# Attention scores of a latent-attention step: the fifth product of four heads as four 64-row matmuls in a row, with four score banks and two banks for turned probabilities

## The reference, cut to what matters

```
def mla_attend(q_abs, q_r, q_pos, ckv, kr, k_pos):
    s = (jnp.einsum('bqhr,bkr->bhqk', q_abs, ckv).astype(jnp.float32)
         + jnp.einsum('bqhp,bkp->bhqk', q_r, kr).astype(jnp.float32)) * SOFTMAX_SCALE
    mask = q_pos[:, None] >= k_pos[None, :]
    s = jnp.where(mask[None, None], s, NEG_INF)
    p = jax.nn.softmax(s, axis=-1).astype(ckv.dtype)
    return jnp.einsum('bhqk,bkr->bqhr', p, ckv)
```

## Time and profile before

| | us |
|---|---|
| median of 3 runs (2332.59 to 2333.3) | 2333.02 |
| the profiled execution | 2344.84 |
| its span | 2343.0 |
| PE busy (94% of the span) | 2205.3 |
| DVE busy (56%) | 1308.4 |
| ACT busy (43%) | 1002.9 |
| score matmuls (L842), 1600 of them, busy | 359.8 |
| value matmuls (L861), 816, busy | 211.5 |
| transposes (L852), 1088, busy | 137.6 |

### The profile page before, as it was taken

How to read it: one execution, slowest core, us unless ns; L and a number is a source line. 1 busy time by engine, 2 the same in 40 slices (tenths; PEclk the granted TensorE clock), 3 DMA queues, 4 the chain that set the end, 5 groups by cost and what they waited for, 6 DMA issues and landing times.

```text
span 2343.0 us, 33629 instructions
## 1 busy us (share of the span) xinstructions
PE 2205.3 (94%) x12021; PEld 2036.9 (87%) x12021; DVE 1308.4 (56%) x2647; ACT 1002.9 (43%) x1802; POOL 364.7 (16%) x500
## 2 busy tenths in 40 slices
PE   5999599999999998786999999999999999999997
PEld 4888478888888887665999999999999999999997
DVE  4565477788777776332644455444644464446445
ACT  3555456555555544322433343334333443344333
POOL 1333221111000010101400050004100420023001
PEclk9999799999999999887999999999999999999999
DMA  5454432111110010404453434443453345344533
GB/s 171 150 162 145 118 81 55 41 35 34 28 28 28 19 64 5 166 1 156 129 176 119 142 118 157 145 137 119 135 166 121 128 136 174 106 150 134 175 117 131
DMA packets 134866, 257.99 MB, mean 110 GB/s; under 512 B 18682, under 2 KB 84482, under 8 KB 133430
## 3 DMA queue, kind: packets, MB, share of 16 engines
q1 hardware_dynamic: 111454, 223.29, 29.3%
q10 hardware_dynamic: 20960, 20.19, 2.9%
q0 software_dynamic: 2304, 12.58, 1.4%
HBM read 213.45 MB, written 42.79 MB: 109 GB/s over the span
## 4 chain that ended last, share of the span: by engine, by line
PE 51%; DVE 1%; issue 1%; DMA 0%; ACT 0%; POOL 0%; DVEq 0%; POOLq 0%; SPq 0%; ACTq 0%
PE d_ps L112 50%; PE d_ps L1567 1%; DMA d_hf<-out_ht 0%; DVE d_gate_p L1518 0%; DVE d_mrg L80 0%; POOL d_fstat L1389 0%; DVE d_y L1481 0%; ACT d_mrg L1347 0%; ACT d_zs L1375 0%; DVE d_ya L1522 0%; DVE d_ht L80 0%; ACT d_ht L1293 0%; DVE d_pool L80 0%; DVE d_y L1556 0%; DVE d_y L1483 0%
## 5 line engine op out<-in xcount | busy, mean ns | idle before, releaser
L112 PE MATMUL d_ps<-d_ht,d_wr 128*128 128x412 f32 x3840 | 737.4, 350 | 22.2 <-DVE d_ht L80 22.1
L112 PEld LDWEIGHTS d_ps<-d_ht,d_wr 128*128 128x128 f32 x3840 | 718.3, 188 | 26.2 <-issue 22.6
L80 DVE TENSOR_TENSOR d_wr<-d_ws,d_wr 128x1024 fp32r<-128x1024 f32 x262 | 322.9, 1232 | 553.4 <-ACT d_wr L1288 553.3
L1288 ACT ACTIVATE d_wr<-d_ws 128x1024 fp32r<-128x1024 f32 x262 | 277.5, 1059 | 608.2 <-PE d_ps L112 598.9
L842 PE MATMUL b_ps<-kt,b_qs 128*128 128x512 f32 (+3 forms) x1600 | 359.8, 377 | 18.6 <-POOL b_qs L80 13.8
L842 PEld LDWEIGHTS b_ps<-kt,b_qs 128*128 128x128 f32 x1600 | 278.3, 195 | 65.2 <-POOL b_qs L80 14.3
L861 PE MATMUL b_ps<-b_pt,kv 128*128 128x512 f32 x816 | 211.5, 402 | 8.7 <-DVE b_pt L80 8.7
L80 DVE TENSOR_TENSOR b_pt<-b_ps,b_pt 128x512 fp32r<-128x512 f32 x272 | 171.9, 683 | 83.0 <-ACT b_pt L746 82.6
L739 ACT ACTIVATE b_p<-b_p,b_bias 128x1024 f32<-128x1024 f32 (+7 forms) x192 | 172.0, 898 | 103.8 <-DVE b_low L797 100.4
L746 ACT ACTIVATE b_pt<-b_ps 128x512 fp32r<-128x512 f32 x272 | 143.8, 596 | 146.6 <-PE b_ps L852 146.3
L861 PEld LDWEIGHTS b_ps<-b_pt,kv 128*128 128x128 f32 x816 | 153.6, 191 | 48.3 <-DVE b_pt L80 14.1
(11 more groups left out here) (193 smaller groups left out, 2289.4 us busy)
## 6 DMA issues: line engine op xcount, KB each, us to landing
d_ws<-in_w SPq DMA_DIRECT2D x264, 512.0 KB, 3.5
out_q<-a_qout SPq DMA_DIRECT2D x17, 768.0 KB, 3.3
d_hf<-out_ht SPq DMA_DIRECT2D x26, 412.0 KB, 3.5
a_x<-in_x ACTq DMA_DIRECT2D x17, 512.0 KB, 3.8
out_ht<-a_hf SPq DMA_DIRECT2D x17, 512.0 KB, 4.2
d_olf<-out_olat SPq DMA_DIRECT2D x42, 206.0 KB, 2.9
b_qf<-out_q SPq DMA_DIRECT2D x32, 256.0 KB, 2.8
b_qf<-out_q SPq DMA_DIRECT2D x128, 64.0 KB, 2.6
```

The source lines that it names most:

```text
L80: return e.tensor_tensor(low, source, high.bitcast(f32), ALU.subtract)
L112: mm = pe.matmul(out, stationary(a, k), moving(b, k), start=first and k == 0 and a + b == 0, stop=last and k == depth - 1 and a == 1)
L1288: act.activation(wr[k % 2][:, 0, :, :], ws[k % 4][:, :, :], ACT.Copy).then_inc(w_hi, 1)
```

## The change

Three things go together.

- The rotary high x low product, pair (2,3), is taken out of the head's step. After the fourth head's four matmuls of a chunk, four matmuls of 64 rows follow, one for each head, each into its own head's bank. Heads 0 and 2 use rows 0 to 63, heads 1 and 3 rows 64 to 127. POOL lays the low parts of heads 1 and 3 into the other half for that (three splits instead of two). The low x low part of the sum is left out.
- The scores of a unit go chunk after chunk, and within a chunk head after head. A bank is finished only with the last of the four 64-row matmuls, which counts `s_ok` up by four; each eviction waits for that.
- The banks are dealt anew: four for scores, two for turned probabilities. `attend_orders` makes its lists from these numbers and costs: for the planner a head's step is four matmuls, the fourth head's step six.

```diff
-NS, NTB, NPT = 3, 3, 4
+NS, NTB, NPT = 4, 2, 4
...
-    scores = [("S", u, h, c) for u in range(units) for h in range(HG) for c in range(chunks(u))]
+    scores = [("S", u, h, c) for u in range(units) for c in range(chunks(u)) for h in range(HG)]
...
         if kind == "S":
-            return 5 * max(0.107, 0.0535 * width(u, step[3], 4))
+            return (4 + 2 * (step[2] == HG - 1)) * max(0.107, 0.0535 * width(u, step[3], 4))
...
         if kind == "C":
-            out = [("S", u, *at)]
+            out = [("S", u, HG - 1, at[1])]
...
                 pool.wait_ge(q_half, u + 1)
-                split(pool, qs[u % 2][ROPE:P, 2, :, :], qf[u % 2][ROPE:P, 1, :, :],
-                      qs[u % 2][ROPE:P, 2, :, :]).then_inc(q_ok, 1)
+                split(pool, qs[u % 2][ROPE:P, 2, 0:HG:2, :], qf[u % 2][ROPE:P, 1, 0:HG:2, :],
+                      qs[u % 2][ROPE:P, 2, 0:HG:2, :])
+                split(pool, qs[u % 2][0:ROPE, 2, 1:HG:2, :], qf[u % 2][0:ROPE, 1, 1:HG:2, :],
+                      qs[u % 2][0:ROPE, 2, 1:HG:2, :]).then_inc(q_ok, 1)
...
-                    dve.wait_ge(s_ok, n + 1)
+                    dve.wait_ge(s_ok, number["S", u, HG - 1, c] + 1)
...
-                    pairs = ((0, 0), (0, 2), (1, 0), (2, 1), (2, 3))
+                    pairs = ((0, 0), (0, 2), (1, 0), (2, 1))
                     for k, (a, b) in enumerate(pairs):
-                        mm = pe.matmul(ps_s[n % NS][:, 0:keys * P], q[:, a, h, :], kt[:, first:first + keys, b, :],
-                                       start=k == 0, stop=k == len(pairs) - 1)
-                    mm.then_inc(s_ok, 1)
+                        pe.matmul(ps_s[n % NS][:, 0:keys * P], q[:, a, h, :], kt[:, first:first + keys, b, :],
+                                  start=k == 0, stop=False)
+                    if h == HG - 1:
+                        for head in range(HG):
+                            rows = slice(ROPE * (head % 2), ROPE * (head % 2) + ROPE)
+                            mm = pe.matmul(ps_s[(n - h + head) % NS][:, 0:keys * P], q[rows, 2, head, :],
+                                           kt[rows, first:first + keys, 3, :], start=False, stop=True)
+                        mm.then_inc(s_ok, HG)
```

## The result

The changed kernel takes 2392.01 us (median of 4 runs, 2391.38 to 2394.55) against 2333.16 us before: 58.9 us more, a ratio of 1.025 with a 95% interval of 1.024 to 1.027. The forecast was 2397 in a range of 2363 to 2430.

A forecast was written before the change was run, and what follows sets the result against it. PE was taken to bound the attention stage. Halves -14, products' wait +50, score banks' wait +25 and clock +3 sum to +64 us on the median of 2333.0: 2397 us, range 2363 to 2430.

The forecast's parts named there:

- PE bounds the stage, and the change would turn its full time into waits: Attention stage: PE busy 654.8 of 690 us; the stage gets some 64 us longer and nothing else moves.
- The price of a bare pair of tiles, 1.14 us: Two tiles transposed, then multiplied with nothing between: PE waits 1.14 us, with a period of about 3.4 us.
- The wait before the products, +50: PE waits for turned probabilities before value products: +50 us, ends +32 and +76.
- The cause given to it, two banks: Two instead of three banks for turned probabilities were said to cause the +50 us wait before value products.
- The count of 36 bare pairs: In the changed program order, 36 of 136 pairs of tiles have transposes followed at once by their products.
- The wait for score banks, +25: Four banks filled together delay evictions, so PE waits where score groups touch: +25 us, ends +16 and +36.
- The halves, -14: 64-row score matmuls on alternate row halves partly run side by side: -14 us, ends 0 and -28.
- The term of zero for changing: Entering and leaving the 64-row matmuls was taken to cost nothing, judged by the decode stage; other end +26 us.
- rival C: 64-row matmuls run one behind the other, or each mode change empties the array: 2411 or 2437 us; chance 22%.
- Scaled probabilities, 0: PE's 16.9 us wait for normalised probabilities in the attention stage was left as it is.
- The clock, +3: More idle times on PE may slow its clock: +3 us, allowed 0 to +10.
- GpSimd's third split: Extra split on POOL, mostly covered by its long waits for ACT; only the first unit's could show, up to +1 us.

The follow-up runs named there:

- the new lists: Only the planner's durations, signal time and queue ranks changed, separately for each kernel: changed kernel 2313.86 us, kernel before 2304.25 us.

## Why the prediction was right, point by point

- **PE bounds the stage, and the change would turn its full time into waits.** Right. The stage is 57 us longer and the rest of the program the same.
- **The price of a bare pair of tiles, 1.14 us.** Right: 1.14 at the stage's end, with a period of 3.51 us where 3.4 stood.
- **The wait before the products, +50.** It is +41 (55.2 - 14.1), within the ends of 32 and 76. 62 waits of 0.89 us on average, where 60 of 1.5 and 0.4 were taken, 64 us in all. The addition for ACT or DVE being late was too high: of the 39 waits that show at the products themselves five were 1.3 to 1.75 us beyond the modelled end, but most were the bare 0.97.
- **The cause given to it, two banks.** This step failed, though the number held. The heading and the text laid the +50 on NTB = 2. The runs put banks alone at +19 us, the scores' order alone at +25, both at +65. The count of 36 bare pairs was right as a reading of the list, but the prediction didn't ask what made the list so. That the sum held in spite of this is owed to the list being given: whatever made the bare pairs, they were there to be counted. With another list, the same two banks let the products wait 0.7 us.
- **The wait for score banks, +25.** It is +31 (37.3 - 6.0), within the ends of 16 and 36. The part for `b_p` is 28 waits of 1.1 us, where 20 of 1.4 and 14 of 0.2 were taken. That finishing four heads together makes this wait holds (10.5 us for `b_p` with separate finishing, 31.8 with joint). That the kernel is slower by as much does not: joint finishing with its list costs 3.3 us, while the products' wait shrank by 23.
- **The halves, -14.** It is -9.4, and -7.5 with the new lists. It lies within the ends, but the -14 was half of two ends and not a mechanism, so that it came near is luck. Side by side the four save 0.46 us a group, and changing in and out takes back all but 0.07 where products follow. The term of zero for changing was wrong: 0.19 us at each change. The row of the decode stage, a change in the number of columns, said nothing on a change in the number of rows. *The Trainium skill says in "TensorEngine Tiling (Array Packing)", Key Properties, that changing the tiling mode drains the engine; the traces agree in so far as each change costs 0.19 us. The Trainium skill's rule in "TensorE: Matmul & The Clock Gate", Part 3, that matmuls on different row groups run at the same time, agrees too: the two starts of a pair are 3 to 5 ns apart. Both together had given about -2.* It is more, since behind 17 groups a wait hides the way out, and before transposes a change costs 0.15 us. Of rival C the first half is out: the four half matmuls span 0.66 us, not 0.9. Its second half, a price for each change, is real, but smaller than what the pairs save.
- **Scaled probabilities, 0.** It is -6: the transposes wait 10.6 us where they waited 16.9. The wait of 5.8 us at 917.6, behind the last scores, is gone, and all five that are left lie before 333 us; the likely reason is that tiles of the unit before now stand there, among the 30 after the last scores. Not foreseen.
- **The clock, +3.** Not told apart. The stage's granted clock was 0.97 in both.
- The sum of the parts that were measured, 41.1 + 31.3 - 9.4 - 6.3 + 1.8 (first queries, 14.3 to 16.1 us) = 58.5 us, where the stage is 57.1 longer. It is rough to some us: waits at weight loads are not quite PE's loss, and the 1.8 are no sign of GpSimd's third split, since the run with banks alone, which has two, waits 15.6.
- Of the 58.9 us, 49 go away with new lists for both kernels (78 - 29), and 9.6 stay.

## What to carry to other kernels

Where lists are made once and followed by waiting, a change of banks or order is two changes, the structure and the list that a rough planner makes of it. Here the lists were worth 78 us on one kernel and 29 on the other, and the structure about 10. Before judging a structure, give each its own fitting lists: read the planner's durations and its allowance between engines from the trace (the way out of a matmul belongs to the allowance), and see that a tile's chain runs beside other tiles' work. Matmuls of half the rows should stand together in pairs and in as long a row as possible, since each change of rows cost 0.19 us here, against 0.23 us saved by each pair; four in a row barely paid, and a longer row wasn't tried.

## What the runs showed of the hardware

Two 64-row matmuls of 512 columns on different halves of the rows run side by side: four took 0.66 us, 1.13 on one half, 0.94 with all 128 rows. Within a pair the starts are 3 to 5 ns apart. A change between 128 and 64 rows costs about 0.19 us each way, half in the step at it and half in the step behind it, and the first weight load of the new kind comes 0.35 us late. Two pairs alone lie wholly within these steps (0.33 us each); what a pair costs in a longer row, no run shows. A change from 128 to 64 columns in the decode stage shows no such gap.
